# Larger place tiles and earlier expert loads, quarters moved from GpSimd to VectorE, and smaller batches at both ends of a long gather, in a two-block transformer kernel

## The chip, the core and the metric

The kernel runs on one core of one Trainium2 chip, as one program. The metric is device time in microseconds, taken by the clock of the chip. Five engines work side by side: TensorE (PE in the profile, with its weight loads as PEld), VectorE (DVE), ScalarE (ACT), GpSimd (POOL) and SyncE (SP, here used only to issue DMAs). Each engine takes its own instructions strictly in the order in which they are written, and waits where a semaphore has not reached its value.

## The reference

Two transformer blocks on 256 tokens of width 1024, one layer each, everything in fp32. What matters here is the second half of each block.

```python
# block 1: hierarchical mixture of experts, 4 groups of 8 experts, 2 experts for each token
h = h + hierarchical_moe(rmsnorm(h), ...)
#   for each expert e: silu(x @ w_gate[e]) * (x @ w_up[e]) @ w_down[e], weighted by the token's gate
#   w_gate, w_up: 32 x 1024 x 512, w_down: 32 x 512 x 1024  (2 MB each, 192 MB in all)
x = rmsnorm(h, final_norm_g)
...
# block 2, last part: product keys pick 16 of 16384 experts for each of 8 heads of a token
q = (xt @ w_q); s = q . sub_keys; top 16 of each half, then top 16 of the 256 sums
act = gelu(x . u_tab[expert]); out = sum_k gate_k * act_k * v_tab[expert_k]
```

The last part reads 128 rows of `u` and of `v` (4 KB each) for each of the 256 tokens.

## The kernel before

The program is written engine by engine, and the order on an engine is the order of the text. There are five stages: `mixers_*` (block 1's attention and gating), `experts_*` (its experts), `mixers2_*` and `cross_*` (block 2 up to the cross attention), and `peer_*` (its product key experts). Nothing is scheduled by a planner. Each stage has counters (`m_pe`, `p_dve` and so on), and a wait names a step of a counter.

**Weights.** Each piece of weights is a 2 MB load into one of seven slots of 16 KB for each partition (`piece`, `load_piece`, L138 to L171). Pieces have a fixed order, `load_order`; SP issues them, and waits first for the piece `behind` places earlier to have landed, so that two or three are under way. `high_quarters` (ScalarE, L173 to L178) rounds a piece to fp32r in four quarters of 1024 columns, and `low_quarters` (L180 to L185) takes the rest, raw minus rounded, on VectorE or on GpSimd. A product of fp32 accuracy is then three fp32r products (`three`).

**Experts.** At most 64 tokens use an expert, each in a slot. `PG` holds, for the four experts of a group of four, a 0/1 matrix from tokens to slots. For each of the 32 experts TensorE runs gate (32 matmuls of 256 columns in two halves of the array), up (the same), the sums of the expert before into the tokens (`add`), the slots' gates (`gate_of_slots`), two transposes of the hidden values, the turned `PG`, for the first 28 experts a part of the next group's gather, and down (`y`). VectorE copies the slots' gates (L841), multiplies silu by up (L843, `h`) and splits; ScalarE does silu (L732), the copy `hp` (L734) and the scaled result `ysh` (L738). Pieces are `eg`, `eu`, `ed` (gate, up, down) for each expert; expert piece j goes into the slot that piece j-7 leaves, so SP also waits for TensorE's step of piece j-7. The first seven are issued once TensorE has finished the mixers (`r11`). `b0` to `b3` are the first pieces of block 2. `b0` waits for step `y29` and for `eu31` to have landed, `b1` for `gate30` and `ed31`. The quarters of `b0` are rounded around the work on expert 31.

**Product key experts.** `select(n)` on VectorE finds the 32 experts of the two heads n%4 of token half n//4; its outer sums are L1922, and its result `idx{n}` (L1955). TensorE computes 16 query units `q0` to `q15` (4 for each of `pq0` to `pq3`), each 24 matmuls, and keys from them. A gather g (GpSimd, L2045) fetches for each of 128 tokens row `IDX[:, g]` of `uv` (8 KB, 1 MB in all) into one of 14 places of a ring. Gather 2 waits for `q7`, 6 for `q11`, 12 for `q15`, and a gather that reuses a place for the row that lay there to have been summed; gathers 8 to 11 reuse the places of 0 to 3. For each batch of four rows VectorE takes the dot products (`dots`, L1892), ScalarE gelu (L1808), weights (L1813) and diagonal matrices (`DG`, L1819), and TensorE adds the rows (`add_rows_pe`, two fp32 matmuls of 512 columns for each row). Batch 0 is added between `q11` and `q12`, all others after `q15`. After the last row come a norm and the stores.

## Time and profile before

| | us |
|---|---|
| median of 3 runs (1681.23 to 1686.05) | 1681.42 |
| profiled execution, its own time | 1684.5 |
| its span | 1682.7 |
| TensorE busy | 1468.9 (87%) |
| VectorE busy | 790.7 (47%) |
| ScalarE busy | 465.2 (28%) |
| bytes read from HBM | 541.87 MB, 323 GB/s over the span |

The chain that ended last has 54% of its time on PE and 24% on DMA. These shares are an average over stages with different limits: the experts run from 155.7 to 630.5 us of the span, the gather stage from about 1003 us to the end, and what binds differs. A row of a timeline gives the start, the time to the end of the group, engine, line, tiles, how many instructions were merged, and in brackets the idle time before it and who ended that.

### The profile page before, as it was taken

Reading aid. Unit: us, or ns where it says so; the run is one execution under the profiler, and the core shown is the slowest. Engines: PE = TensorE matmul, PEld = TensorE weight load, DVE = VectorE, ACT = ScalarE, POOL = GpSimd, SP = SyncE. Lnnn points to the kernel's source line nnn. Section 1 sums busy time; section 2 is a strip of 40 time slices with the busy share of each in tenths; the row PEclk is TensorE's granted clock in tenths of the full one; section 3 lists DMA queues with packets and bytes.
Section 4 is the critical chain, followed back from the end, with each engine's and each line's share of the span. In section 5 each row is a group of like instructions: output and inputs, shape, how many; then the busy total and the mean of one; then the engine's idle time right before and its main releaser. Section 6 shows DMA issues by size and latency. Waiting matters only on the chain.

```text
span 1682.7 us, 19564 instructions
## 1 busy us (share of the span) xinstructions
PE 1468.9 (87%) x7830; PEld 903.3 (54%) x7830; DVE 790.7 (47%) x1821; ACT 465.2 (28%) x1173; POOL 271.6 (16%) x280
## 2 busy tenths in 40 slices
PE   7998999999999989999999888878787777877776
PEld 7777555555555549976668686333332333333332
DVE  5535111111111125256464476576776677545443
ACT  4621100110101024355533443222222222222221
POOL 0001000000000000000000033433333333433330
PEclk8999999999999999989999998989989998999998
DMA  8209999999999983522234218999999999999993
GB/s 341 101 1 398 425 426 425 424 424 425 427 423 425 424 352 115 214 102 100 101 150 150 110 67 325 422 421 422 422 420 423 421 422 421 421 422 423 422 421 162
DMA packets 63055, 544.24 MB, mean 323 GB/s; under 512 B 6384, under 2 KB 6896, under 8 KB 10096
## 3 DMA queue, kind: packets, MB, share of 16 engines
q1 hardware_dynamic: 25664, 273.31, 39.4%
q0 software_dynamic: 36864, 268.45, 38.5%
q8 instruction: 63, 1.03, 0.2%
q10 hardware_dynamic: 432, 1.18, 0.2%
q14 instruction: 32, 0.26, 0.0%
HBM read 541.87 MB, written 1.05 MB: 323 GB/s over the span
## 4 chain that ended last, share of the span: by engine, by line
PE 54%; DMA 24%; DVE 9%; issue 8%; ACT 4%; POOL 1%; SPq 0%; ACTq 0%; DVEq 0%; POOLq 0%
PE PS L189 52%; DMA AR<-in_uv,CO 19%; DMA Wk<-in_uv,CO 4%; DVE AR L1892 2%; PE PS L199 2%; ACT Wk L1813 1%; DMA CO<-in_const 1%; DVE AR L843 1%; ACT AR L1819 0%; DVE AR L1922 0%; DVE XL L259 0%; DVE Wk L1892 0%; DVE Wk L841 0%; DVE LO L185 0%; ACT XH L252 0%
## 5 line engine op out<-in xcount | busy, mean ns | idle before, releaser
L189 PE MATMUL PS<-AR 128*64 128x256 f32 (+3 forms) x2784 | 633.2, 463 | 122.0 <-ACT AR L1819 120.3
L189 PEld LDWEIGHTS PS<-AR 128*64 128x64 f32 (+3 forms) x2784 | 308.6, 160 | 449.8 <-issue 227.8
L1892 DVE CUSTOM_DVE_ANT_0 AR<-AR,PS 128x1024 f32<-128x1024 f32 x218 | 263.6, 1219 | 199.7 <-DMA AR<-in_uv,CO 199.1
L2045 POOL DMA_INDIRECT AR<-in_uv,CO x218 | 207.5, 952 | 336.1 <-PE PS L189 327.3
L280 POOL TENSOR_TENSOR ST<-ST 128x2 f32<-128x2 f32 (+3 forms) x12 | 10.3, 860 | 904.1 <-DVE ST L263 904.1
L189 PE MATMUL PS<-AR,Wk 128*64 128x512 f32 (+4 forms) x592 | 148.7, 565 | 4.3 <-ACT Wk L734 1.4
L185 DVE TENSOR_TENSOR LO<-AR,HI 128x1024 fp32r<-128x1024 f32 x100 | 118.0, 1232 | 64.1 <-ACT HI L178 64.1
L189 PE MATMUL PS<-Wk,AR 128*64 128x256 f32 (+2 forms) x488 | 113.7, 451 | 20.8 <-ACT AR L1819 20.2
L1808 ACT ACTIVATE Wk<-Wk 128x4 f32<-128x4 f32 x64 | 13.1, 205 | 423.6 <-DVE Wk L1892 423.6
L189 PE MATMUL PS<-XH,HI 128*128 128x256 f32 x352 | 104.0, 295 | 10.3 <-DVE XL L259 7.0
L178 ACT ACTIVATE HI<-AR 128x1024 fp32r<-128x1024 f32 x104 | 102.5, 1053 | 16.1 <-PE PS L189 9.4
L841 DVE COPY Wk<-PS 128x1 f32<-128x1 f32 x32 | 5.1, 158 | 211.0 <-PE PS L189 211.0
L189 PE MATMUL PS<-XL,HI 128*128 128x256 f32 x352 | 101.4, 288 | 0.0
L189 PE MATMUL PS<-XH,LO 128*128 128x256 f32 x352 | 101.2, 288 | 0.0
L189 PEld LDWEIGHTS PS<-Wk,AR 128*64 128x64 f32 (+1 forms) x488 | 56.5, 164 | 75.6 <-issue 38.2
L189 PEld LDWEIGHTS PS<-AR,Wk 128*64 128x64 f32 (+2 forms) x592 | 53.9, 151 | 77.9 <-issue 68.0
L189 PE MATMUL PS<-HI,XH 128*128 128x512 f32 (+1 forms) x208 | 85.0, 409 | 3.8 <-ACT AR L1303 2.7
L1819 ACT ACTIVATE AR<-CO,Wk 128x128 f32<-128x128 f32 x256 | 81.8, 390 | 2.1
L189 PE MATMUL PS<-LO,XH 128*128 128x512 f32 (+1 forms) x208 | 82.0, 394 | 0.0
L189 PE MATMUL PS<-HI,XL 128*128 128x512 f32 (+1 forms) x208 | 81.8, 393 | 0.0
L189 PEld LDWEIGHTS PS<-XH,HI 128*128 128x128 f32 x352 | 69.4, 197 | 11.9 <-DVE XL L259 6.9
L851 DVE SCALAR_TENSOR_TENSOR YL<-PS,Wk,YH 128x512 fp32r<-128x512 f32 x32 | 24.0, 750 | 110.1 <-ACT YH L738 110.1
(263 smaller groups left out, 1684.8 us busy)
## 6 DMA issues: line engine op xcount, KB each, us to landing
AR<-in_w_gate SPq DMA_DIRECT2D x28, 2048.0 KB, 13.1
AR<-in_w_up SPq DMA_DIRECT2D x27, 2048.0 KB, 14.1
AR<-in_w_down SPq DMA_DIRECT2D x27, 2048.0 KB, 14.7
AR<-in_w_in SPq DMA_DIRECT2D x15, 2048.0 KB, 9.9
Wk<-in_w_up SPq DMA_DIRECT2D x5, 2048.0 KB, 14.7
Wk<-in_w_down SPq DMA_DIRECT2D x5, 2048.0 KB, 14.7
AR<-in_w_out SPq DMA_DIRECT2D x4, 2048.0 KB, 8.0
Wk<-in_w_gate SPq DMA_DIRECT2D x4, 2048.0 KB, 12.8
```

Source lines behind the costliest of these rows:

```text
L178: act.activation(hi[:, cs], w[:, cs], ACT.Copy).then_inc(*steps.up(f"{name}.{k}"))
L185: eng.tensor_tensor(lo[:, cs], w[:, cs], hi[:, cs].bitcast(F32), ALU.subtract).then_inc(*steps.up(f"{name}.{k}"))
L189: return pe.matmul(o, l, r, start=start, stop=stop, skip_group_check=True)
L199: return pe.transpose(o, i, ident[0:n, 0:n])
L280: pool.tensor_tensor(ST[:, a:b], ST[:, a:b], HALF[:, 0:b - a], ALU.pow).then_inc(*rms.up(site))
L843: dve.tensor_tensor(HM[:, b, :], SG[:, b, :], P(4 + b)[:, 256:512], ALU.mult).then_inc(*m_dve.up(f"h{ex}"))
L851: dve.scalar_tensor_tensor(YL[:, b, :], P(6), SLOT_GATE[:, b:b + 1], YH[:, b, :].bitcast(F32), ALU.mult, ALU.subtract).then_inc(*m_dve.up( ...
L1808: act.activation(GEL[:, cs], DT[:, cs], ACT.Gelu).then_inc(*a_own.up())
L1813: t = act.activation(WT[:, g:g + 1], BGf[:, g:g + 1], ACT.Copy, scale=GEL[:, g:g + 1])
L1819: act.activation(DG[:, g % 8, :], ident, ACT.Copy, scale=WT[:, g:g + 1]).then_inc(diags, 1)
L1892: t = dve.tensor_tensor_reduce(r, r, P(6 if g < 128 else 2, 2), 1.0, 0.0, ALU.mult, ALU.add, DT[:, g:g + 1])
L2045: pool.indirect_dma_start(RING[k], None, uv, bass.IndirectOffsetOnAxis(ap=IDX[:, g:g + 1], axis=0)).then_inc(g_in[k], 16)
```

## The change

Ten edits, in four places.

1. **Loads.** The seven pieces of the mixers use other slots and halves, so that slots come free earlier. `eu0` is issued at step `k3`, `out0` and `out1` one step later than before, `eg0` at `u1`, `eu1` at `turn2.3`, `ed0` and `ed1` at `r01`, `eg1` and `eg2` at `r11`. The expert loop issues from `eu2` on.
2. **Start.** TensorE's spare matmuls wait for the identity matrix, whose rounded copy now lies in `WM`; 20 of them instead of 36 stand first.
3. **Experts.** `PG` holds each expert's 64 slots twice, so that turning it and summing the gates take one matmul of 128 output rows instead of two of 64; the turned `PG` is an fp32r product with the rounded identity instead of an fp32 one. VectorE does `h` before the slots' gates, and down waits for the gates.
4. **Expert 31.** Two quarters of `b0` are rounded between `hp31` and `ysh31` (before: three ahead of silu31, one after `hp31`), two after `ysh31`. Of the rests, two stand ahead of `ys31` and two after block 2's first scaling.
5. **Gather stage.** The rests of `pq2` move from GpSimd to VectorE, behind `select(0)`; `exp0` moves from behind `q7`'s keys to behind `q11`'s, and `gates0` behind the first batch of dots. Batches are 2, 2, 61 times 4, 2, 2, 1, 1, 1, 1 rows instead of 64 times 4.

```diff
-            piece(name, src, n % 4, n % 2)
+            piece(name, src, (2, 3, 0, 1, 2, 0, 1)[n], (n + 1) % 2)
...
-            sp.wait_ge(*a_pe.at("k3"))
-            load_piece(sp, "out0")
-            sp.wait_ge(*a_pe.at("v1"))
-            load_piece(sp, "out1")
+            for name, step in (("eu0", "k3"), ("out0", "v1"), ("out1", "g1"), ("eg0", "u1"), ("eu1", "turn2.3"), ("ed0", "r01"),
+                               ("ed1", "r01"), ("eg1", "r11"), ("eg2", "r11")):
+                sp.wait_ge(*a_pe.at(step))
+                load_piece(sp, name, 2 if name in ("out0", "out1") else len(load_order))
...
-            spare(pe, 6, 36)
+            spare(pe, 6, 20)
...
-            sp.wait_ge(*a_pe.at("r11"))
-            for ex in range(32):
+            for ex in range(2, 32):
...
-                    pg = PG[:, g % 2, tt, k4 * 64:k4 * 64 + 64].bitcast(F32)
-                    for j in range(2):
-                        t = mm(pe, G[64 * j:64 * j + 64, 256 + tt * 128:384 + tt * 128], pg, ident, True, True)
+                    t = mm(pe, G[:, 256 + tt * 128:384 + tt * 128], twice(PG[:, g % 2, tt, k4]), WMt[:, 0:128], True, True)
...
                 if ex == 31:
-                    act.wait_ge(*m_pe.at("gate31"))
-                    high_quarters(act, "b0", b_act, range(3))
...
-                    high_quarters(act, "b0", b_act, range(3, 4))
+                    high_quarters(act, "b0", b_act, range(2))
                 act.wait_ge(*m_pe.at(f"y{ex}"))
                 act.activation(YH[:, b, :], P(6), ACT.Copy, scale=SLOT_GATE[:, b:b + 1]).then_inc(*m_act.up(f"ysh{ex}"))
+            high_quarters(act, "b0", b_act, range(2, 4))
             high_quarters(act, "b1", b_act)
...
-            low_quarters(pool, "pq2", p_act, p_pool)
...
+            low_quarters(dve, "pq2", p_act, p_dve)
             low_quarters(dve, "pq3", p_act, p_dve)
             dots(dve)
+            gates(dve, 0)
...
+        SIZES = [2, 2] + [4] * 61 + [2, 2, 1, 1, 1, 1]
+        STARTS = [sum(SIZES[:b]) for b in range(len(SIZES) + 1)]
```

On TensorE in the first expert, behind the gate and up matmuls: the slots' gates (`Wk,PG`), the two transposes (L199), the turned `PG`, the gather and down. Before:

```order
L189 MATMUL PS<-Wk,PG 64x1 x4
L199 MATMUL PS<-CO,AR 128x128 [waits m_dve]
L199 MATMUL PS<-CO,AR 128x128
L189 MATMUL PS<-CO,PG 64x128 x4
L189 MATMUL PS<-PG,XGH 128x256 [waits m_dve]
```

After:

```order
L189 MATMUL PS<-Wk,PG 128x1 x2
L199 MATMUL PS<-CO,AR 128x128 [waits m_dve]
L199 MATMUL PS<-CO,AR 128x128
L189 MATMUL PS<-WM,PG 128x128 x2
L189 MATMUL PS<-PG,XGH 128x256 [waits m_dve]
```

Two of four instructions are gone in each of two places, and the turned tile reads `WM` instead of `CO`.

On ScalarE around expert 31 (L732 and after L730 are silu, L734 and L732 `hp`, L738 and L736 `ysh`; `HI_49` is `b0`, `HI_50` is `b1`; ring0 and ring1 are their landings). Before:

```order
L178 ACTIVATE HI_49<-AR 128x1024 [waits ring0,m_pe]
L178 ACTIVATE HI_49<-AR 128x1024 x2
L732 ACTIVATE AR<-PS 128x256 [waits m_pe]
L734 ACTIVATE Wk<-PS 128x256 [waits m_pe]
L178 ACTIVATE HI_49<-AR 128x1024 [waits ring0]
L738 ACTIVATE YH<-PS,Wk 128x512 [waits m_pe]
L178 ACTIVATE HI_50<-AR 128x1024 [waits ring1]
L178 ACTIVATE HI_50<-AR 128x1024 x3
```

After:

```order
L730 ACTIVATE AR<-PS 128x256 [waits m_pe]
L732 ACTIVATE Wk<-PS 128x256 [waits m_pe]
L178 ACTIVATE HI_49<-AR 128x1024 [waits ring0]
L178 ACTIVATE HI_49<-AR 128x1024
L736 ACTIVATE YH<-PS,Wk 128x512 [waits m_pe]
L178 ACTIVATE HI_49<-AR 128x1024 [waits ring0]
L178 ACTIVATE HI_49<-AR 128x1024
L178 ACTIVATE HI_50<-AR 128x1024 [waits ring1]
L178 ACTIVATE HI_50<-AR 128x1024 x3
```

The first wait for `b0` stands behind `hp31` now, and two quarters stand ahead of `ysh31`.

On ScalarE in the gather stage, from the keys of `q7` on (L1838 and after L1841 copy keys, L1848 and L1851 queries, L1824 and L1827 are `exp0`, `HI_49` is `pq3`). Before:

```order
L1838 ACTIVATE AR<-PS 128x2x128 [waits p_pe] x2
L1824 ACTIVATE RW<-RW 128x32 [waits p_dve]
L178 ACTIVATE HI_49<-AR 128x1024 [waits ring3]
L178 ACTIVATE HI_49<-AR 128x1024 x3
L1848 ACTIVATE RW<-PS 128x256 [waits p_pe] x2
L1838 ACTIVATE AR<-PS 128x2x128 [waits p_pe]
```

After:

```order
L1841 ACTIVATE AR<-PS 128x2x128 [waits p_pe] x2
L178 ACTIVATE HI_49<-AR 128x1024 [waits ring3]
L178 ACTIVATE HI_49<-AR 128x1024 x3
L1851 ACTIVATE RW<-PS 128x256 [waits p_pe] x2
L1841 ACTIVATE AR<-PS 128x2x128 [waits p_pe]
```

`exp0`, which waits for VectorE's `sub0`, no longer stands ahead of the quarters of `pq3` and of the copies of `q8` and `q9`.

## Rows read from the trace of the kernel before

**Rows 1.** Busy time by stretch: span, engines (instructions), granted clock, DMA share, GB/s.

```profile
200.00:300.00 100.00, 95.88 (x780) 57.29 (x778) 18.99 (x46) 9.51 (x20) 0.00 (x0) 1.00 1.01 426
```

**Rows 2.** Timeline of PE, inside one expert's period.

```profile
413.90 0.40 PE L189 MATMUL PS<-Wk,PG 128*64 128x1 f32 x8
414.89 0.51 PE L199 MATMUL PS<-CO,AR 128*128 128x128 f32 x2 [0.59 <-DVE AR L843]
415.32 0.66 PE L189 MATMUL PS<-CO,PG 128*64 128x128 f32 x8
```

**Rows 3.** Timeline of ACT and of DVE, the same expert.

```profile
412.89 0.39 ACT L732 ACTIVATE AR<-PS 128x256 f32<-128x256 f32 x1 [6.22 <-PE PS L189]
...
414.42 0.41 DVE L843 TENSOR_TENSOR AR<-AR,PS 128x256 f32<-128x256 f32 x1
```

**Rows 4.** Timeline of SP: issues of pieces, first and last of the experts.

```profile
127.32 0.33 SPq L171 DMA_DIRECT2D AR<-in_w_gate  x1
...
135.30 0.33 SPq L171 DMA_DIRECT2D AR<-in_w_gate  x1
...
159.42 0.33 SPq L171 DMA_DIRECT2D AR<-in_w_up  x1
...
603.19 15.32 SPq L171 DMA_DIRECT2D AR<-in_w_in  x4
```

**Rows 5.** Page, groups of instructions: busy us, mean ns, idle before.

```profile
L185 DVE TENSOR_TENSOR LO<-AR,HI 128x1024 fp32r<-128x1024 f32 x100 | 118.0, 1232 | 64.1 <-ACT HI L178 64.1
...
L178 ACT ACTIVATE HI<-AR 128x1024 fp32r<-128x1024 f32 x104 | 102.5, 1053 | 16.1 <-PE PS L189 9.4
```

**Rows 6.** Timeline of PE and of DVE, end of the experts.

```profile
621.52 3.65 PE L189 MATMUL PS<-Wk 128*64 128x512 f32 x16 [0.48 <-ACT Wk L734]
626.75 0.50 PE L189 MATMUL PS<-YH,PT 64*128 64x512 f32 x2 [1.57 <-DVE YL L851]
...
627.99 2.48 DVE L857 TENSOR_TENSOR Hs<-PS,Hs 128x512 f32<-128x512 f32 x4 [1.29 <-PE PS L189]
```

**Rows 7.** Timeline of POOL and of DVE around the selection of the first experts.

```profile
984.73 9.55 POOL L185 TENSOR_TENSOR LO<-AR,HI 128x1024 fp32r<-128x1024 f32 x4 [20.78 <-ACT HI L178]
...
986.82 7.49 DVE L1922 TENSOR_TENSOR AR<-CO 128x32 f32<-128x32 f32 x7
...
1031.99 0.68 DVE L1922 TENSOR_TENSOR AR<-CO 128x32 f32<-128x32 f32 x7
```

**Rows 8.** Timeline of POOL, gathers 0, 2 and 12.

```profile
1003.15 1.17 POOL L2045 DMA_INDIRECT Wk<-in_uv,CO  x1 [8.88 <-DVE RW L1956]
...
1006.54 1.96 POOL L2045 DMA_INDIRECT AR<-in_uv,CO  x1 [0.30 <-issue]
...
1042.30 0.94 POOL L2045 DMA_INDIRECT AR<-in_uv,CO  x1 [11.44 <-PE PS L189]
```

**Rows 9.** Timeline of ACT and of PE between keys 7 and batch 0.

```profile
996.88 0.38 ACT L1838 ACTIVATE AR<-PS 128x256 f32<-128x256 f32 x1 [0.36 <-PE PS L189]
1002.99 0.23 ACT L1824 ACTIVATE RW<-RW 128x32 f32<-128x32 f32 x1 [5.72 <-DVE RW L1956]
...
1016.05 0.38 ACT L1848 ACTIVATE RW<-PS 128x256 f32<-128x256 f32 x1 [2.48 <-PE PS L189]
...
1020.83 5.40 PE L189 MATMUL PS<-Wk,AR 128*128 128x512 f32 x8 [3.62 <-ACT AR L1819]
```

**Rows 10.** Timelines of DVE, ACT and PE at the last rows.

```profile
1662.93 1.22 DVE L1892 CUSTOM_DVE_ANT_0 AR<-AR,PS 128x1024 f32<-128x1024 f32 x1 [1.23 <-DMA AR<-in_uv,CO]
...
1664.43 0.85 ACT L1813 ACTIVATE Wk<-RW,Wk 128x1 f32<-128x1 f32 x4
...
1655.92 7.13 PE L189 MATMUL PS<-AR 128*128 128x512 f32 x16 [1.12 <-ACT AR L1819]
1665.77 8.83 PE L189 MATMUL PS<-AR 128*128 128x512 f32 x16 [2.71 <-ACT AR L1819]
...
1674.64 1.29 DVE L1976 TENSOR_TENSOR Hs<-PS,Hs 128x512 f32<-128x512 f32 x2 [10.48 <-PE PS L189]
```

More of the change, by code:

```diff
@@ L576, in program @@
         XG = w2(4096, "p (b c n) -> p b c n", b=2, c=8)
-        PG = rounded("PG", "Wk", wk.at, 1024)[:, :].rearrange("p (b t n) -> p b t n", b=2, t=2)
-        wk(1024)
+        PG = rounded("PG", "Wk", wk.at, 2048)[:, :].rearrange("p (b t e d s) -> p b t e d s", b=2, t=2, e=4, d=2)
+        wk(2048)
+        twice = lambda v: v.rearrange("p d s -> p (d s)")
         HP = wk(512, "p (b n) -> p b n", b=2)
@@ L690, in experts_pe @@
                 for tt in range(2):
-                    pg = PG[:, g % 2, tt, k4 * 64:k4 * 64 + 64].bitcast(F32)
-                    for j in range(2):
-                        t = mm(pe, G[64 * j:64 * j + 64, 256 + tt * 128:384 + tt * 128], pg, ident, True, True)
+                    t = mm(pe, G[:, 256 + tt * 128:384 + tt * 128], twice(PG[:, g % 2, tt, k4]), WMt[:, 0:128], True, True)
                 t.then_inc(*m_pe.up(f"turned{ex}"))
@@ L790, in places_dve @@
             b = g % 2
-            slot = bc(io[:, 0:64].unsqueeze(1), [128, 4, 64])
+            slot = bc(io[:, 0:64].unsqueeze(1).unsqueeze(1), [128, 4, 2, 64])
             for tt in range(2):
-                pg = PG[:, b, tt, :].rearrange("p (e s) -> p e s", e=4)
-                dve.tensor_tensor(pg, slot, bc(RK[:, tt, 4 * g:4 * g + 4].unsqueeze(2), [128, 4, 64]), ALU.is_equal).then_inc(
+                own_slot = bc(RK[:, tt, 4 * g:4 * g + 4].unsqueeze(2).unsqueeze(3), [128, 4, 2, 64])
+                dve.tensor_tensor(PG[:, b, tt], slot, own_slot, ALU.is_equal).then_inc(
                     *m_dve.up(f"pg{g}.{tt}"))
@@ L837, in experts_dve @@
                     places_dve(dve, g + 1)
-                if ex == 31:
-                    low_quarters(dve, "b0", b_act, b_dve, range(2))
+                dve.wait_ge(*m_act.at(f"silu{ex}"))
+                dve.tensor_tensor(HM[:, b, :], SG[:, b, :], P(4 + b)[:, 256:512], ALU.mult).then_inc(*m_dve.up(f"h{ex}"))
                 dve.wait_ge(*m_pe.at(f"gsum{ex}"))
                 dve.tensor_copy(SLOT_GATE[:, b:b + 1], P(5 - b)[:, 0:1]).then_inc(*m_dve.up(f"gs{ex}"))
-                dve.wait_ge(*m_act.at(f"silu{ex}"))
-                dve.tensor_tensor(HM[:, b, :], SG[:, b, :], P(4 + b)[:, 256:512], ALU.mult).then_inc(*m_dve.up(f"h{ex}"))
                 dve.wait_ge(*m_act.at(f"hp{ex}"))
@@ L848, in experts_dve @@
                 if ex == 31:
-                    low_quarters(dve, "b0", b_act, b_dve, range(2, 4))
+                    low_quarters(dve, "b0", b_act, b_dve, range(2))
                 dve.wait_ge(*m_act.at(f"ysh{ex}"))
@@ L1362, in mixers2_dve @@
             scaled(dve, XZ[:, 1, :], H[:, 1, :], ST[:, 1:2]).then_inc(*b_dve.up("xs1"))
+            low_quarters(dve, "b0", b_act, b_dve, range(2, 4))
             turn_dve(dve, X2, sm["g_nmix"], b_act, b_dve, "x")
@@ L1691, in program @@
         p_act = Steps(sem("p_act"), [*p_act_names, *[f"exp{n}" for n in range(1, 8)]])
-        p_dve = Steps(sem("p_dve"), ["ss", "mean", "xs1", *eights("x"), "idx0", "sub0", "gates0", *split_steps("pq3"),
+        p_dve = Steps(sem("p_dve"), ["ss", "mean", "xs1", *eights("x"), "idx0", "sub0", *split_steps("pq2"), *split_steps("pq3"), "gates0",
                                      *[f"{k}{n}" for n in range(1, 8) for k in ("idx", "sub", "gates")]])
-        p_pool = Steps(sem("p_pool"), split_steps("pq2"))
         ld_sk, ld_gp, ld_fin, st_out = sem("ld_sk"), sem("ld_gp"), sem("ld_fin"), sem("st_out")
@@ L1753, in peer_sp, with batch @@
             sp.wait_ge(st_out, 48)
+        SIZES = [2, 2] + [4] * 61 + [2, 2, 1, 1, 1, 1]
+        STARTS = [sum(SIZES[:b]) for b in range(len(SIZES) + 1)]
+        def batch(b):
+            return range(STARTS[b], STARTS[b + 1])
         def sums_at(tt, j):
@@ L1758, in add_rows_pe @@
         def add_rows_pe(pe, b):
-            for g in range(4 * b, 4 * b + 4):
+            for g in batch(b):
                 tt, n = g // 128, g % 128
@@ L1800, in peer_pe @@
                     add_rows_pe(pe, 0)
-            for b in range(1, 64):
+            for b in range(1, len(SIZES)):
                 add_rows_pe(pe, b)
         def weights_act(act, b):
-            cs = slice(4 * b, 4 * b + 4)
+            cs = slice(STARTS[b], STARTS[b + 1])
             act.wait_ge(dotted, b + 1)
             act.activation(GEL[:, cs], DT[:, cs], ACT.Gelu).then_inc(*a_own.up())
-            if b % 8 == 0:
-                act.wait_ge(*p_dve.at(f"gates{b // 8}"))
+            act.wait_ge(*p_dve.at(f"gates{(STARTS[b + 1] - 1) // 32}"))
             act.wait_ge(*a_own.at())
-            for g in range(4 * b, 4 * b + 4):
+            for g in batch(b):
                 t = act.activation(WT[:, g:g + 1], BGf[:, g:g + 1], ACT.Copy, scale=GEL[:, g:g + 1])
@@ L1815, in weights_act @@
             act.wait_ge(*a_own.at())
-            for g in range(4 * b, 4 * b + 4):
+            for g in batch(b):
                 if g >= 8:
@@ L1851, in peer_act @@
                 keys(hc)
-                if ui == 1:
+                if ui == 2:
                     exp_act(act, 0)
-                if ui == 2:
                     weights_act(act, 0)
-            for b in range(1, 64):
+            for b in range(1, len(SIZES)):
                 if b in DOTTED_AT_SUB:
@@ L1888, in dots @@
             b = batches.count
-            for g in range(4 * b, 4 * b + 4):
+            for g in batch(b):
                 r = RING[place_of[g]][:, 0:1024]
@@ L2007, in peer_dve @@
             mean(dve, ST[:, 40:41], D).then_inc(*e_dve.up("mean0"))
-            while batches.count < 64:
+            while batches.count < len(SIZES):
                 dots(dve)
```

23 lines of the change are left out of this document (12 added, 11 removed).

## The prediction

> **What bounds the kernel now.** I read the busy table by stretches first, since the whole span mixes several limits. In a stretch of 100 us inside the experts TensorE is busy for 95.9 us at the full granted clock, and the 16 DMA engines are busy throughout (share 1.01) at 426 GB/s [rows 1]. So two limits lie on each other: a change that shortens TensorE's work gains only until the transfers bind. Next I read TensorE's timeline inside one expert for the parts that are not weights [rows 2], then SP's issues, which tell when pieces land [rows 4]. At the end of the experts the two are apart: the last piece, `ed31`, landed at 608.2 us (`b1` waits for it; the four issues from 603.19 on are 5.0 us apart), while TensorE began the product with it only at 621.52 and ended at 625.2 [rows 4, 6]. TensorE binds there, with 13 us of cover over the transfers. In the gather stage the page's rows are of DMA: 256 gathers of 1 MB, each 2.5 us, so what counts is when the stream starts, whether it has a gap near its start, and how long the tail behind the last row is. The start hangs on `idx0`, and just ahead of it stands the row that surprised me: seven small outer sums took 7.49 us on VectorE, and the same seven take 0.68 us in the next selection. They end with GpSimd's four quarters (984.73 + 9.55 = 994.28 against 986.82 + 7.49 = 994.31) [rows 7].
>
> The sums are made in the profiled execution: span 1682.7, own time 1684.5, against a median of 1681.42. I take differences from its span and put them on the median.
>
> **Experts, TensorE's side.** The slots' gates are 0.40 us for eight instructions, four calls; two calls are left, so I take 0.2 off. TensorE then waits 0.59 for `h` before the transposes; `h` could start when silu is done (412.89 + 0.39 = 413.28) but stood behind the gates' copy until 414.42 [rows 2, 3]. With the order turned, `h` runs 413.3 to 413.7, ahead of the end of the slots' gates at 414.1, and the wait goes; next late there is nothing but TensorE itself. The turned `PG` starts at 415.32 and what follows it comes 0.59 later; two fp32r calls should cost between nothing less (0.59, if an fp32r product of 128 columns is as slow as four fp32 calls) and 0.12; I take 0.2, so 0.4 off, nearer to the fp32r rows. Sum 1.2 us for each expert, bounds 0.8 and 1.3, times 32 = 38 us (25 to 42). This alone would end the experts at 625.2 - 38 = 587. The wait of down for the gates' copy costs nothing: VectorE does it right behind `h`, and the copy `hp` takes as long.
>
> **Experts, the transfers' side.** From the landing of the first piece (135.30, 8.0 after its issue) to that of the last (608.2) are 95 pieces in 472.9 us, 4.98 us each [rows 4]. Early loads cannot run further ahead than seven slots. Before, the seventh piece was landing when TensorE gave its first slot back (159.42, step `gate0`) [rows 4], and the stream did not pause. After, the seven lie ready and the stream rests until that step: the eighth piece lands 8.0 after it, at 167.4, and the last, 88 pieces on, at 167.4 + 88 x 4.97 = 604.8. I add 0.3 for the start: twice two place tiles of 512 columns instead of 256 on the way to the first gather are some +0.6 (bounds 0 and 0.8), and the spare matmuls, which begin later but end nearer to the first weights, I take at -0.3 (bounds -2 and +1). So `ed31` lands at 605.1 instead of 608.2. All the loading early is worth 3 us; the mixers' own later loads of `out0` and `out1` are hidden, since each is issued some 10 us ahead of its first quarter and lands in 8. TensorE (587) is ahead of it, so in the last third TensorE waits for pieces, and **the transfers bind**.
>
> **The end of the experts.** `y31` would end at about 609. But `b0` lands 5.0 behind `ed31`, at 610.1, and ScalarE now waits for it between `hp31` and `ysh31`. Two quarters at 1.0 [rows 5] give 612.1, `ysh31` 612.8; VectorE's two quarters at 1.2 (from 611.1) end at 613.5, `ys31` at 614.2; the last sums take 1.2 at the full clock, and at half of it 2.3 (TensorE has idled for 5 us; the row before shows full clock behind an idle of 1.57 [rows 6]); I take 2.3. Then four additions of 2.48 [rows 6] end at 619.1 against 630.5. **Gain 11.4 us** (12.5 with the full clock; 14 if `b0` did not stand in the way; 9 if pieces take 5.0). The two quarters of `b0` behind `ysh31` and `b1`, which lands at 615.1, end on ScalarE at 619.0, just in time for the norm. The two rests behind the first scaling take 2.4 and fit an idle of 3 us of VectorE's there.
>
> **Start of the gathers.** GpSimd's quarters go. If they held the outer sums, `idx0` comes 7.49 - 0.68 = 6.8 us earlier, at 996.2, and gather 0 is issued at 996.4 instead of 1003.15 [rows 7, 8]. VectorE does the eight rests (9.3 us) by 1005.5. `q8` starts with the first of them at 997.4, `q11` is 13.5 later at 1010.9 instead of 1016.0 [rows 9]: before, the copy of `q8` stood behind `exp0`, which waited for VectorE until 1002.99, and behind four quarters. Batch 0's rows on TensorE start at 1015.3 instead of 1020.83; `exp0`, the table load and `gates0` now stand between, some 3 us; two rows take 5.4 of a cold clock, where four took 8.8 [rows 9]. So they end at 1020.7 instead of 1029.7, and `q15` is done at 1033.1 instead of 1042.1. **But the stream does not go on then**: gather 10 reuses the place of row 2, and row 2 is in batch 1 now, which TensorE adds only after `q15`. I put row 2 at 1037.5 to 1039.0, so gather 10 is issued about 4.0 ahead of where gather 12 was (1042.30 [rows 8]); two gathers more stand behind the gap, +5.0, and a load of 0.5 MB that fell into the restart has passed, -1.2. Sum -0.2, bounds -1.5 and +2. I take **0**. From there the stream is as before.
>
> **The tail.** The last dot starts at 1662.93; four weights are 0.85, and the last 16 matmuls start at 1665.77 and take 8.83 (7.13 where the idle before was short) [rows 10]. With single rows, the diagonal of the last is ready at about 1665.1, but TensorE must first be done with the rows before: it needs 1.8 for a row and they come every 2.5. Counting from the batch ahead of the last eight, it runs without pause and ends at 1667.4 (that batch at the full clock) to 1669.2 (cold). Against 1674.6: **gain 6.3 us** (5.4 to 7.2). What follows is unchanged.
>
> Sum: -11.4 + 0 - 6.3 = **-17.7**, 1681.4 - 17.7 = **1663.7 us**.
>
> **A rule weighed against the trace.** The row of the outer sums shows a VectorE instruction with two inputs in SBUF that lasts as long as a GpSimd one beside it [rows 7]. The Trainium skill, SBUF — State Buffer, "Who interferes with whom", states that such an instruction contends with a GpSimd instruction that reads SBUF; here the trace agrees, 7.49 against 0.68 us. The same page ("SBUF: two separate sides") warns that GpSimd, locked out, cannot write the descriptors of its own DMAs; by it moving the quarters to VectorE starves the first gathers, which is the second rival below. Its list of consequences exempts `tensor_tensor` from that as inferred.
>
> **Rivals.**
> *A. The transfers do not bind; TensorE does* (the fp32r products bring nothing and the wait for `h` stays in part). Then the experts gain 32 times the saving. At 0.3 us that is 10 us less the 2 of the late `ysh31`: total about -14, 1667. Against it: `h` is free 0.8 us before it is needed. 0.07.
> *B. The first gathers are starved by VectorE's rests.* GpSimd's issue took 1.17 and 1.96 us beside four rests, 0.94 alone [rows 8]: slowed, not stopped. If they wait until the rests end (1005.5), gather 1 lands some 8 us later, at 1014, batch 0 is dotted at 1015, its rows start 4 us later and so does everything behind: -13.7, 1667.7. 0.08.
> *C. The outer sums stay long, or the restart behind gather 10 is slower.* The start is then up to 7 us worse: -11, 1671. 0.10.
> *D. More than forecast*: no cold clock at the last sums, pieces at 4.93: -21.5, 1660 or below. 0.15.
> *E. Slower than before: the granted clock falls in the experts.* Once the transfers bind, TensorE waits some 1.4 us in every expert, some 14 times. In the gather stage a wait of 2.71 went with 8.83 instead of 7.13 [rows 10]. Each us at half clock costs 0.5, and 1.5 us of slack for each expert absorbs 3. From 6 us of half clock in each of 14 experts (14 x (3.0 - 1.5) = 21) the gain is gone, and at half clock throughout (14.9 of 14.9, 14 x 6 = 84) the kernel takes 1748. Against it: waits of 1.12 did not lower it [rows 10], and a TensorE that falls behind no longer waits. 0.03.
> *F. The change does not do what it says in full*: the transfers' gain is lost again before the gathers, and only the tail stays: -6, 1675; or a place wait that I missed eats that too, 1681. 0.05.
>
> **How the numbers follow.** The forecast has 0.52, with 1659 to 1668. The range reaches over B to most of C and D: 1657 to 1671. A measurement of this kernel tells 0.3% (5 us) from no change. Faster by more than that, below 1676.4: the forecast, A, B, C, D and half of F, 0.945, of which I take 0.065 off for what I have not seen: 0.88. Within: the other half of F, 0.025, and 0.045 of that, 0.07. Slower: E and the rest, 0.05.
>
> **What would show it.** Right: in the first half of the experts a period of about 13.6 us on TensorE, in the last third 14.9 with waits for a DMA of about 1.4; the first half-rounding of `b0` near 610 with `ysh31` behind it, and the residual additions at 619; seven outer sums in 0.7; the first gather at 985 (996.4 - 11.4); a gap of the stream after gather 9; the last rows in pieces of 1.8. Wrong: no waits for pieces, a clock below 1.00 among the experts, the first gather's issue far behind `idx0`, or a second gap in the stream.

## The result, and the profile after

| | before | changed |
|---|---|---|
| runs beside each other, median (lowest to highest) | 1683.2 us (1681.23 to 1686.05, 4 runs) | 1666.92 us (1664.19 to 1670.09, 4 runs) |
| ratio, 95% interval | | 0.991 (0.9889 to 0.9931) |
| span of the profiled execution | 1682.7 | 1666.0 |

The changed kernel is 16.3 us faster by the medians and 16.7 by the profiled spans. The forecast was 17.7 less.

The busy table by stretches of the changed kernel, with the columns of [rows 1] (busy of PE, PEld, DVE, ACT and POOL, granted clock, DMA share, GB/s):

```profile
140.00:150.00 10.00, 9.33 (x55) 8.99 (x54) 5.96 (x53) 2.62 (x9) 0.00 (x0) 0.69 0.00 0
200.00:300.00 100.00, 100.00 (x772) 60.69 (x770) 20.96 (x47) 10.18 (x21) 0.00 (x0) 1.00 1.01 426
400.00:500.00 100.00, 92.33 (x690) 54.02 (x691) 20.38 (x45) 9.80 (x20) 0.00 (x0) 1.00 1.01 424
...
1015.00:1020.00 5.00, 5.00 (x45) 5.00 (x43) 4.86 (x24) 0.77 (x2) 0.00 (x0) 1.00 0.54 200
1020.00:1025.00 5.00, 4.97 (x42) 4.72 (x40) 4.79 (x10) 1.53 (x4) 0.00 (x0) 1.00 0.02 6
1025.00:1030.00 5.00, 3.43 (x6) 1.47 (x5) 3.45 (x8) 4.56 (x16) 0.00 (x0) 0.68 0.29 104
1030.00:1035.00 5.00, 5.00 (x13) 2.15 (x12) 0.00 (x0) 2.11 (x3) 2.95 (x4) 0.98 0.54 174
```

In the first half of the experts TensorE is busy throughout, in the second half it is busy for 92 of 100 us, at the same full clock and the same transfer rate. It waits for pieces now. Two stretches have idle transfers: 140 to 150, where the seven early pieces lie ready, and 1015 to 1035, the gap behind gather 9.

TensorE's timeline of the changed kernel: two transposes of successive experts in the first half (start, us, tiles), and gate and up of one expert in the second half, with the wait for `eu`.

```profile
207.06 0.47 PE L199 MATMUL PS<-CO,AR 128*128 128x128 f32 x2
220.72 0.46 PE L199 MATMUL PS<-CO,AR 128*128 128x128 f32 x2
...
419.75 3.62 PE L189 MATMUL PS<-AR 128*64 128x256 f32 x32
424.25 3.67 PE L189 MATMUL PS<-AR 128*64 128x256 f32 x32 [0.88 <-DMA AR<-in_w_up]
```

The period is 13.66 us instead of 14.77, and the wait of 0.59 for `h` [rows 2] is gone. From the seventeenth expert on it is 14.7 to 14.8, with three of 15.3 to 15.8, and most experts wait 0.8 to 1.2 us for a DMA (two of them 1.4 and 1.9).

To see where the time went, I cut each profiled execution at four events: the start of the first expert's gate on TensorE, the first scaling of block 2 on VectorE (the one behind the residual additions), the issue of gather 0 on GpSimd, and the start of the last dot. The stretches between them are differences of starts in the timelines.

```
us                to gate0   to scaling   to gather 0   to last dot   to the end   span
before             155.7       477.1        370.3         659.8         19.8      1682.7
changed            158.0       466.8        362.2         666.6         12.4      1666.0
n_late_loads       158.5       467.1        364.7         665.6         13.7      1669.6
n_old_turn         161.6       467.9        360.9         665.3         13.7      1669.3
n_old_turn_h       161.3       476.1        362.9         666.0         13.7      1679.9
n_b0_late          156.2       467.0        365.1         665.8         13.7      1667.8
n_pool_rests       157.7       466.3        367.4         661.4         12.4      1665.1
n_first4           155.8       468.0        361.3         663.2         13.8      1662.1
n_gate8            158.3       466.8        361.3         659.5         13.8      1659.6
n_tail4            161.2       466.2        364.7         665.8         18.2      1676.0
n_b0_b1_late       157.7       463.3        365.5         665.7         12.4      1664.6
n_old_start        158.2       465.9        358.9         665.1         13.7      1661.8
n_best             156.0       463.3        363.5         657.7         12.4      1653.0
n_best_start       155.8       463.2        365.6         658.0         13.5      1656.0
```

The table is read by column. A stretch in which two kernels have the same program still differs by up to 6 us in the first column (155.8 to 161.6 for the kernels with the changed start), by some 3 either way in the third, and by 1.4 in the last, all in single executions. The experts and the stream of gathers, which hang on transfers, repeat within about 2 us. So an effect of the experts is read from the second column and one of the gathers from the fourth, not from the spans.

### The profile page after: what moved, and what is told of

Same layout as the page of the kernel before. It is cut to its first block, busy times and chain, and to the rows that moved or that the text cites. A ratio compares the mean times of both kernels' runs of the same rounds, so it can differ in the third digit from the quotient of the medians.

```text
span 1666.0 us, 18993 instructions
## 1 busy us (share of the span) xinstructions
PE 1451.0 (87%) x7494; PEld 893.6 (54%) x7494; DVE 794.8 (48%) x1826; ACT 467.1 (28%) x1178; POOL 262.3 (16%) x276
## 4 chain that ended last, share of the span: by engine, by line
DMA 46%; PE 35%; issue 8%; DVE 6%; ACT 4%; POOL 1%; SPq 0%; ACTq 0%; DVEq 0%; POOLq 0%
PE PS L189 34%; DMA AR<-in_uv,CO 23%; DMA AR<-in_w_up 17%; DMA Wk<-in_uv,CO 3%; DMA Wk<-in_w_up 3%; DVE AR L1894 1%; PE PS L199 1%; ACT Wk L1816 1%; DMA CO<-in_const 1%; DVE LO L185 1%; DMA AR<-in_w_in 1%; POOL AR L2047 1%; ACT AR L1822 1%; DVE XL L259 0%; ACT Wk L1812 0%
## 5 line engine op out<-in xcount | busy, mean ns | idle before, releaser
L185 DVE TENSOR_TENSOR LO<-AR,HI 128x1024 fp32r<-128x1024 f32 x104 | 122.5, 1232 | 64.9 <-ACT HI L178 64.9
L1812 ACT ACTIVATE Wk<-Wk 128x4 f32<-128x4 f32 (+2 forms) x69 | 14.1, 205 | 423.7 <-DVE Wk L1894 423.7
L838 DVE TENSOR_TENSOR AR<-AR,PS 128x256 f32<-128x256 f32 x32 | 13.5, 421 | 201.7 <-ACT AR L730 201.7
L178 ACT ACTIVATE HI<-AR 128x1024 fp32r<-128x1024 f32 x104 | 102.5, 1053 | 17.2 <-DMA AR<-in_w_in 10.5
L730 ACT ACTIVATE AR<-PS 128x256 f32<-128x256 f32 x32 | 12.3, 384 | 231.1 <-PE PS L189 231.1
## 6 DMA issues: line engine op xcount, KB each, us to landing
AR<-in_w_gate SPq DMA_DIRECT2D x28, 2048.0 KB, 14.7
AR<-in_w_up SPq DMA_DIRECT2D x27, 2048.0 KB, 14.7
AR<-in_w_down SPq DMA_DIRECT2D x27, 2048.0 KB, 14.7
Wk<-in_w_up SPq DMA_DIRECT2D x5, 2048.0 KB, 14.7
Wk<-in_w_down SPq DMA_DIRECT2D x5, 2048.0 KB, 14.7
Wk<-in_w_gate SPq DMA_DIRECT2D x4, 2048.0 KB, 14.7
```

The costliest lines, as they stand in the source:

```text
L178: act.activation(hi[:, cs], w[:, cs], ACT.Copy).then_inc(*steps.up(f"{name}.{k}"))
L185: eng.tensor_tensor(lo[:, cs], w[:, cs], hi[:, cs].bitcast(F32), ALU.subtract).then_inc(*steps.up(f"{name}.{k}"))
L730: act.activation(SG[:, b, :], G[:, 0:256], ACT.Silu).then_inc(*m_act.up(f"silu{ex}"))
L838: dve.tensor_tensor(HM[:, b, :], SG[:, b, :], P(4 + b)[:, 256:512], ALU.mult).then_inc(*m_dve.up(f"h{ex}"))
L1812: act.activation(GEL[:, cs], DT[:, cs], ACT.Gelu).then_inc(*a_own.up())
```

## The experiments

Each is the changed kernel with one more edit. Where only one execution was taken, the verdict rests on its stretches.

**The early loads (n_late_loads).**

```diff
-            for name, step in (("eu0", "k3"), ("out0", "v1"), ("out1", "g1"), ("eg0", "u1"), ("eu1", "turn2.3"), ("ed0", "r01"),
-                               ("ed1", "r01"), ("eg1", "r11"), ("eg2", "r11")):
+            for name, step in (("out0", "v1"), ("out1", "g1"), ("eg0", "r11"), ("eu0", "r11"), ("ed0", "r11"), ("eg1", "r11"), ("eu1", "r11"),
+                               ("ed1", "r11"), ("eg2", "r11")):
...
-                load_piece(sp, name, 2 if name in ("out0", "out1") else len(load_order))
+                load_piece(sp, name, 2 if name in ("out0", "out1") else 3)
```

> The changed kernel, but all seven first expert pieces are issued when TensorE has finished the mixers, in their order, each when the piece three places earlier has landed; the mixers' slots stay as changed. Theory of the resting stream: in the changed kernel the seven pieces lie ready by 138 us and the transfers then rest until the first slot comes free at 161.7, so the last expert piece lands at 608.7. With the loads from 127.8 on, the first lands at 135.8, the stream does not pause, and the last lands at 135.8 + 95 x 4.97 = 607.9: the residual additions end at 621.5 to 622.5 as before (622.4), the total is within 1 us. Rival (the term of 3 us that the prediction gave the early loads): the additions end at 625.4 and the kernel is 3 us slower than the changed one.

SP's issues of pieces in the changed kernel, from the eighth on, and ScalarE's first rounding of `b0`, which waits for it to land; then the first and the eighth issue of this kernel and the same rounding:

```profile
161.71 0.33 SPq L171 DMA_DIRECT2D AR<-in_w_up  x1
165.16 0.38 SPq L171 DMA_DIRECT2D AR<-in_w_down  x1
171.37 0.33 SPq L171 DMA_DIRECT2D AR<-in_w_gate  x1
...
230.94 0.33 SPq L171 DMA_DIRECT2D AR<-in_w_up  x1
...
613.67 2.00 ACT L178 ACTIVATE HI<-AR 128x1024 fp32r<-128x1024 f32 x2 [3.60 <-DMA AR<-in_w_in]
```

```profile
127.55 0.33 SPq L171 DMA_DIRECT2D AR<-in_w_gate  x1
...
162.21 0.33 SPq L171 DMA_DIRECT2D AR<-in_w_up  x1
...
614.56 2.00 ACT L178 ACTIVATE HI<-AR 128x1024 fp32r<-128x1024 f32 x2 [3.67 <-DMA AR<-in_w_in]
```

Loading the seven pieces some 8 to 83 us earlier moved the landing of `b0` from 614.56 to 613.67. Counted from the first expert's start the scaling comes at 466.8 and at 467.1. The early loads alone are worth 0.3 to 0.9 us, which is less than the column's own scatter. The span of this kernel is 3.6 us longer, as the rival had it, but only 0.3 of that is in the experts; the rest is in stretches with the same program (0.5 at the start, 2.5 ahead of gather 0, 1.3 at the end, less 1.0 in the stream). What sets the end of the stream is the first slot that TensorE gives back (161.71, 162.21), and ahead of it the transfers either rest or have just enough to do.

**TensorE's savings (n_old_turn, n_old_turn_h).** The first turns `PG` by an fp32 product again, the second also puts the slots' gates ahead of `h`.

```diff
-                    t = mm(pe, G[:, 256 + tt * 128:384 + tt * 128], twice(PG[:, g % 2, tt, k4]), WMt[:, 0:128], True, True)
+                    t = mm(pe, G[:, 256 + tt * 128:384 + tt * 128], twice(PG[:, g % 2, tt, k4]).bitcast(F32), ident, True, True)
```

> The changed kernel, but the turned place tile is again an fp32 product with the identity (two instructions). Theory that the transfers bind the experts: TensorE's period in the first experts goes from 13.65 to 13.8 or 13.9 us, still under the 14.9 that three pieces take, and the additions end at 622.4 as in the changed kernel. Rival, that TensorE binds: 32 x 0.2 = 6 us later, 628.

> The changed kernel with the fp32 turned place tile and with the old order on VectorE (the slots' gates ahead of h). Theory: the period of TensorE becomes 13.65 + 0.2 + 0.6 = 14.45; TensorE then is nearly as slow as the transfers, y31 ends at 158.0 + 28 x 14.45 + 4 x 13.9 = 618, the additions end at 624.5 instead of 622.4 and the kernel is 2 us slower. If the wait for h were worth nothing: 622.4. If TensorE bound in full (1.1 us x 32, as before the change): the additions end at 630 or more.

Transposes of two successive experts, n_old_turn and then n_old_turn_h:

```profile
211.31 0.46 PE L199 MATMUL PS<-CO,AR 128*128 128x128 f32 x2
225.19 0.46 PE L199 MATMUL PS<-CO,AR 128*128 128x128 f32 x2
```

```profile
213.50 0.50 PE L199 MATMUL PS<-CO,AR 128*128 128x128 f32 x2 [0.58 <-DVE AR L840]
228.13 0.51 PE L199 MATMUL PS<-CO,AR 128*128 128x128 f32 x2 [0.58 <-DVE AR L840]
```

The periods are 13.88 and 14.63 (14.64 as a mean), against 13.66. So of the 1.11 us saved for an expert, the fp32r product gives 0.22, the order of `h` 0.76, and halving the instructions the rest, 0.13. With 13.88 TensorE still waits for pieces in the last twelve experts, and the scaling comes at 467.9 instead of 466.8: next to nothing. With 14.64 it binds to the end: no expert waits for a piece, and the scaling comes 9.3 later. I had expected 2: the period came out 0.19 above my 14.45, which is 6 us over 32 experts, and the remaining 1 is within the scatter. The order of two VectorE instructions is the part of the change that counts in the experts.

**The end of the experts (n_b0_late, n_b0_b1_late).** The first rounds all of `b0` behind `ysh31` and takes its rests behind the scaling. The second also moves the rounding of `b1` behind the norm's sum of squares.

```diff
-                if ex == 31:
-                    high_quarters(act, "b0", b_act, range(2))
...
-            high_quarters(act, "b0", b_act, range(2, 4))
-            high_quarters(act, "b1", b_act)
+            high_quarters(act, "b0", b_act)
...
             square_sum(act, H[:, 0, :], XS[:, 0, :], ST[:, 0:1]).then_inc(*m_act.up("sq2"))
+            high_quarters(act, "b1", b_act)
```

> The changed kernel, but all four quarters of b0 are rounded behind ysh31, and all its rests are taken behind block 2's first scaling. In the changed kernel ysh31 starts at 615.58, 2.0 after y31 has ended, since ScalarE waits for b0 (landed 613.67) and rounds two quarters; VectorE's rests hold ys31 until 617.04. Theory: ysh31 starts at 613.7, the additions end at 619.8 instead of 622.4; but b1's four quarters now end on ScalarE at 622.6 and the norm's sum of squares stands behind them, so that the normalised residual comes no earlier and the kernel gains 0 to 0.3 us. Rival: b1's quarters are early enough, and the kernel gains 2.6.

> The changed kernel with the four quarters of b0 behind ysh31, as in n_b0_late, and with b1's four quarters moved behind the norm's sum of squares on ScalarE. In n_b0_late the additions ended at 617.2, 461.0 us behind the first expert's start instead of 464.4, but the scaling of the norm started 467.0 behind it, as in the changed kernel (466.8): the gain had been given back to b1's quarters. Theory: now the scaling starts 463.2 to 463.8 behind the first expert's start, and 3 us reach the first gather. Rival: b1's quarters, between the two norms, hold the second norm instead, and nothing is gained.

ScalarE and VectorE at the end of the experts, changed kernel:

```profile
615.58 0.67 ACT L736 ACTIVATE YH<-PS,Wk 128x512 fp32r<-128x512 f32 x1
...
618.71 3.90 ACT L178 ACTIVATE HI<-AR 128x1024 fp32r<-128x1024 f32 x4 [0.57 <-DMA AR<-in_w_in]
...
617.04 0.74 DVE L848 SCALAR_TENSOR_TENSOR YL<-PS,Wk,YH 128x512 fp32r<-128x512 f32 x1
619.96 2.48 DVE L854 TENSOR_TENSOR Hs<-PS,Hs 128x512 f32<-128x512 f32 x4 [2.18 <-PE PS L189]
```

The same in n_b0_late:

```profile
611.99 0.69 ACT L734 ACTIVATE YH<-PS,Wk 128x512 fp32r<-128x512 f32 x1 [3.75 <-PE PS L189]
...
617.27 3.89 ACT L178 ACTIVATE HI<-AR 128x1024 fp32r<-128x1024 f32 x4 [0.81 <-DMA AR<-in_w_in]
621.07 1.04 ACT L266 ACTIVATE XSs<-Hs 128x1024 f32<-128x1024 f32 x1
...
614.76 2.48 DVE L850 TENSOR_TENSOR Hs<-PS,Hs 128x512 f32<-128x512 f32 x4 [1.30 <-PE PS L189]
...
622.23 0.17 DVE L263 TENSOR_SCALAR ST<-ST 128x2 f32<-128x2 f32 x1 [3.71 <-ACT XSs L266]
```

And in n_b0_b1_late, with TensorE behind the experts:

```profile
618.60 1.06 ACT L266 ACTIVATE XSs<-Hs 128x1024 f32<-128x1024 f32 x1 [0.81 <-DVE Hs L849]
...
619.66 3.88 ACT L178 ACTIVATE HI<-AR 128x1024 fp32r<-128x1024 f32 x4
...
626.06 1.15 ACT L1248 ACTIVATE AR<-Hs,ST 128x1024 f32<-128x1024 f32 x1 [1.01 <-POOL ST L280]
...
621.83 9.53 PE L189 MATMUL PS<-WM 128*128 128x256 f32 x58 [5.79 <-issue]
631.19 1.96 PE L199 MATMUL PS<-CO,AR 128*128 128x128 f32 x16
```

In the changed kernel `ysh31` stands behind two roundings, which began at 613.67, when `b0` had landed, and lasted 2.0 us, while `y31` ended at 613.8. Without them the additions begin 458.5 us behind the first expert's start instead of 462.0. But the norm does not: its sum of squares stands behind `b1`'s four quarters and VectorE waits 3.71 us for it. Only when `b1` moves too does the scaling come 463.3 behind the start instead of 466.8, 3.5 us earlier. This is not the gain of the kernel, for the next thing in the way is TensorE. Between the experts and block 2's transposes it has 58 spare matmuls. In the changed kernel they hold the transposes until 634.47, 3.4 us after the normed tokens are ready (631.1); here until 631.19, 4.0 us after (626.06 + 1.15 = 627.2), and in n_best 5.0 us. Counted from the first expert's start, block 2's first product comes at 476.1 here, 477.1 in n_best and 476.0 in n_best_start, and at 476.9 to 479.2 in the kernels that leave `b1` where it is (n_old_turn_h aside): a mean of 1.8 earlier, with ranges that overlap. How much of that reaches gather 0 the executions cannot tell: the stretch behind the scaling was 3.3 longer here than in the changed kernel, 1.3 in n_best and 3.4 in n_best_start. No run here takes the spare matmuls out.

**The rests of `pq2` (n_pool_rests).** `low_quarters(dve, "pq2", p_act, p_dve)` goes back to GpSimd, ahead of its gathers.

> The changed kernel, but the four rests of pq2 are back on GpSimd. Theory, that they hold VectorE's seven outer sums: the sums take 7.5 us instead of 0.68 and the first gather is issued at 993.8 instead of 987.0. q11 comes about 1 later than the changed kernel's, because q8 waits for GpSimd's rests (ready 984.7 to 985, before 993.8), so the restart of the stream behind gather 10, which hangs on q15 and on TensorE, moves by 0 to 2 us and the kernel is only 0 to 2 us slower. Rival: the whole 6.8 us reach the end. Second rival: the outer sums were long for another reason, and stay at 0.68.

The outer sums on VectorE, GpSimd's rests and gather 0 in this kernel; the outer sums and gather 0 in the changed one:

```profile
974.93 7.59 DVE L1925 TENSOR_TENSOR AR<-CO 128x32 f32<-128x32 f32 x7
...
972.83 9.50 POOL L185 TENSOR_TENSOR LO<-AR,HI 128x1024 fp32r<-128x1024 f32 x4 [20.76 <-ACT HI L178]
991.37 1.98 POOL L2048 DMA_INDIRECT Wk<-in_uv,CO  x1 [9.04 <-DVE RW L1959]
```

```profile
977.47 0.68 DVE L1924 TENSOR_TENSOR AR<-CO 128x32 f32<-128x32 f32 x7
...
987.00 1.98 POOL L2047 DMA_INDIRECT Wk<-in_uv,CO  x1 [30.94 <-DVE RW L1958]
```

The seven sums are back at 7.59 us: GpSimd's subtraction of two SBUF tiles did hold them. This is the contention that the Trainium skill (SBUF — State Buffer, "Who interferes with whom") states, and the experiment bears it out. Gather 0 comes 5.2 us later behind the scaling, yet the kernel ends at the same time: 661.4 us from gather 0 to the last dot instead of 666.6. The earlier start is lost in the gap, since ScalarE's copy of `q15`, on which the restart hangs, follows the end of the additions by 401.4 us here (1023.04 - 621.63) and by 401.6 in the changed kernel (1023.99 - 622.44).

**The gap of the stream (n_first4, n_gate8).** In n_first4 the first batch has four rows: `SIZES = [4] * 62 + [2, 2, 1, 1, 1, 1]`. n_gate8 has that too, and:

```diff
-        place_of = [g if g < 8 else g - 8 if g < 12 else ROUND[(g - 12) % 14] for g in range(256)]
+        place_of = [g if g < 8 else ROUND[(g - 8) % 14] for g in range(256)]
...
-                if g in (2, 6, 12):
+                if g in (2, 6, 8):
...
-                if ui == 2:
-                    add_rows_pe(pe, 0)
-            for b in range(1, len(SIZES)):
+            for b in range(len(SIZES)):
```

(gather 8 waits for `q15`, `ROUND` becomes `[*range(8, 14), *range(8)]`, and ScalarE's weights of batch 0 stand behind `q15` as well).

> The changed kernel, but the first two batches of two rows are one of four (as before the change); the small batches at the end stay. Theory: gather 10, issued at 1030.7 in the changed kernel, waits for row 2, which stands behind q15; with four rows in batch 0 gathers 8 to 11 are issued by 1016 and gather 12 at about 1027.8 behind q15, which comes 3.5 later than 1024.0. Gather 12 then lands some 6 us earlier than now, and the kernel is 4 to 6 us faster than the changed one. Rival: the cold clock of the four rows delays q15 so much that nothing is won (0).

> The changed kernel with four rows in batch 0, and in addition batch 0 is added after q15, not between q11 and q12, and gathers 8 to 13 take the six places that q15 frees, instead of 8 to 11 reusing places 0 to 3. Theory: TensorE goes from q11 to q12 without its wait of 3.1 us and without the rows, q15 comes at 1002 + 13.2 = 1015.2 instead of 1024.0, and gather 8 is issued at 1015.5, when gather 7 has just landed: the gap of the stream is 3 to 5 us instead of some 13 of a mean share of one half, gather 14 lands at about 1038 instead of 1046, and the kernel is 8 to 9 us faster than the changed one. Rival: TensorE, which now has eight rows to catch up, holds the places back and opens a second gap; then 4 us or less.

GpSimd's issues around the gap: gathers 9 and 10 of the changed kernel, 11 and 12 of n_first4, 7 and 8 of n_gate8.

```profile
1011.85 0.94 POOL L2047 DMA_INDIRECT Wk<-in_uv,CO  x1 [0.78 <-PE PS L189]
1030.66 0.94 POOL L2047 DMA_INDIRECT AR<-in_uv,CO  x1 [17.87 <-PE PS L189]
```

```profile
1015.10 0.94 POOL L2047 DMA_INDIRECT AR<-in_uv,CO  x1 [0.78 <-PE PS L189]
1027.47 1.16 POOL L2047 DMA_INDIRECT AR<-in_uv,CO  x1 [11.43 <-PE PS L189]
```

```profile
1002.74 0.94 POOL L2044 DMA_INDIRECT AR<-in_uv,CO  x1 [0.30 <-issue]
1015.06 0.94 POOL L2044 DMA_INDIRECT AR<-in_uv,CO  x1 [11.39 <-PE PS L189]
```

Busy table of n_gate8 in the gap:

```profile
1005.00:1010.00 5.00, 5.00 (x45) 5.00 (x44) 4.72 (x14) 1.15 (x3) 0.00 (x0) 1.00 0.93 383
1010.00:1015.00 5.00, 5.00 (x45) 5.00 (x43) 3.65 (x16) 0.94 (x3) 0.00 (x0) 1.00 0.04 18
1015.00:1020.00 5.00, 1.60 (x8) 1.06 (x7) 1.40 (x12) 4.43 (x13) 3.76 (x4) 0.89 0.78 275
```

From gather 0 to the last dot: 666.6 in the changed kernel, 663.2 with four rows (3.4 less; I had expected 4 to 6), 659.5 when nothing stands between `q11` and `q15` (7.1 less; expected 8 to 9). In n_gate8 two stretches of 5 us lack transfers (shares of 0.04 and 0.78), in the changed kernel four (0.54, 0.02, 0.29, 0.54). TensorE catches up with its eight waiting rows without a second gap: GpSimd waits for it once more, 7.43 us ahead of the gather issued at 1050.29, and the DMA share is 1.01 there.

**The last batches (n_tail4).** `SIZES = [2, 2] + [4] * 63`.

> The changed kernel, but the last batches are of four rows again. Theory: the last 16 matmuls start 2.8 us behind the last dot and take 7.1 or 8.8; from the start of the last dot to the end of the span 19.8 us as before the change instead of 12.4, so 7.4 slower (5.7 if they run at the full clock).

TensorE's and VectorE's last work, changed kernel and then n_tail4:

```profile
1636.70 3.70 PE L189 MATMUL PS<-AR 128*128 128x512 f32 x8 [1.12 <-ACT AR L1822]
...
1643.67 14.27 PE L189 MATMUL PS<-AR 128*128 128x512 f32 x32
...
1653.61 1.22 DVE L1894 CUSTOM_DVE_ANT_0 AR<-AR,PS 128x1024 f32<-128x1024 f32 x1 [1.23 <-DMA AR<-in_uv,CO]
...
1657.97 1.29 DVE L1978 TENSOR_TENSOR Hs<-PS,Hs 128x512 f32<-128x512 f32 x2 [3.13 <-PE PS L189]
```

```profile
1650.88 17.00 PE L189 MATMUL PS<-AR 128*128 128x512 f32 x32 [2.80 <-ACT AR L1822]
```

TensorE in n_first4, whose tail takes 13.8 us:

```profile
1631.42 5.40 PE L189 MATMUL PS<-AR 128*128 128x512 f32 x8 [2.81 <-ACT AR L1822]
```

With fours the rest behind the last dot's start is 18.2 us, with single rows 12.4 in four executions and 13.5 to 13.8 in eight others, before the change 19.8. TensorE has no pause in its last 32 matmuls in either. In the changed kernel they take 14.3 us, with a granted clock of 1.00; in n_tail4 they begin behind a wait of 2.80 and take 17.0, with 0.51 and 0.81 in the first two stretches of 5 us. Which of its two values the tail of single rows takes goes with the clock in the batch ahead of the last eight rows: its first eight matmuls took 3.70 us at a granted clock of 1.00 in the changed kernel, and 5.40 at 0.72 in n_first4, and the other executions fall into the same two groups. The single rows are worth 4.4 to 5.8 against n_tail4, whose 5.8 more than the changed kernel is the 5.7 expected for the full clock, and 6.0 to 7.4 against the kernel before.

**The start (n_old_start).** Spare matmuls multiply zeros again, 36 stand first, and the rounded identity lies in the second half of `WM`.

```diff
-            spare(pe, 6, 20)
+            spare(pe, 6, 36)
...
-            dve.tensor_copy(WMt[:, 128:256], zeros)
+            dve.tensor_copy(WMt[:, 0:128], zeros).then_inc(wm_set, 1)
             dve.wait_ge(ld_id, 16)
-            dve.tensor_copy(WMt[:, 0:128], ident).then_inc(wm_set, 1)
+            dve.tensor_copy(WMt[:, 128:256], ident).then_inc(wm_set, 1)
```

> The changed kernel, but the spare matmuls multiply zeros again and 36 of them start first without waiting for the identity; the rounded identity lies in the second half of WM. In all nine profiles with spares on the identity the granted clock is 0.66 to 0.86 between 140 and 150 us, where it was 1.00 before the change, and the first expert starts at 155.8 to 161.6 (before: 155.7). Theory that the spares' start or data lowers the clock: the clock at 140 to 150 is 1.00, the first expert starts at 155.5 to 156.5 plus 0.6 for the wider place tiles, and the kernel is 1 to 3 us faster than the changed one. Rival: the clock falls there by the phase of the stages and does so here too; then the first expert starts at 157 to 161 as in the others and nothing is gained.

The stretch ahead of the first expert in this kernel:

```profile
140.00:150.00 10.00, 9.32 (x54) 8.98 (x53) 5.96 (x53) 2.62 (x9) 0.00 (x0) 0.68 0.02 7
```

The clock is as low as in the changed kernel (0.69), the first expert starts at 158.2, and the ratio to the kernel before is 0.9911 (0.9894 to 0.9927), that of the changed kernel. So it is neither the data nor the start of the spare matmuls. In n_late_loads the transfers ran through this stretch and it was 0.74, so it is not their rest either. TensorE was busy for 3.94 us of the 5 ahead of it (135 to 140) in the kernel before and in the changed one alike. Why the clock falls here in all thirteen executions looked at since the change (0.66 to 0.86) and did not in the one before stays open; with a single execution before, chance is not excluded.

**Together (n_best, n_best_start).** n_best has the edits of n_b0_b1_late and n_gate8; n_best_start has those of n_old_start too.

> The edits of n_b0_b1_late and of n_gate8 together. If they add up: 2.5 to 3.5 us at the end of the experts and 7 in the gather stage, that is 9.5 to 10.5 us less than the changed kernel, 1656 to 1657, ratio to the kernel before 0.984 to 0.986. Rival: the gap before q15 grows by what the experts give, no, q15 moves with them, so I see no way for it; a clock that falls elsewhere can cost 2 to 3.

> n_best with the old start of n_old_start. If the start costs 1 to 3 us, 1654 to 1656; if not, as n_best.

n_best: median 1656.29 (1654.80 to 1659.86, 4 runs) against 1679.47 of the kernel before beside it, ratio 0.9869 (0.9851 to 0.9887). n_best_start: 1658.88, 0.9885 (0.9868 to 0.9901). In the table n_best has both gains in their columns: 3.5 us to the scaling and 8.9 to the last dot. Its interval lies just below that of the changed kernel (0.9889 to 0.9931); the two ratios are 0.4% apart, some 7 us. I had expected 9.5 to 10.5, so the two gains do not add up in full: the 7 us are what n_gate8 alone gave from gather 0 on, and what n_b0_b1_late should add cannot be told from the scatter. The old start adds nothing.

## Why the prediction was right, and where its terms were off

- **Experts, TensorE's side.** 1.2 us for an expert were forecast, 1.11 came. The wait for `h` was the largest part, as said, and nothing took its place. The shares were off in opposite directions: `h` gave 0.76 where I had 0.59, the other edits 0.35 where I had 0.6.
- **Experts, the transfers' side.** That the transfers take over was right, with a period of 14.76 instead of 14.9 and waits of 0.8 to 1.2 instead of 1.4. But they did so from the seventeenth expert on, not only in the last third. The landing was mis-sized: `b0` at 613.7 instead of 610.1. Two things were left out. The eighth piece was issued at 161.7 and not at 159.7, since the first expert started 2.3 later and not 0.3, outside my bounds for the start (-2 and +1.8): TensorE's lower clock between 140 and 150 (0.69) was in no row of before. And the stream did not pick up at full rate: the next slots come free at 165.16 and 171.37, at TensorE's pace. The twentieth piece landed at 230.94 (the issue that waits for it), where 161.7 + 8.0 + 12 x 4.97 = 229.3; 1.6 us were lost there. So the 3 us that I gave to the early loads were not there: n_late_loads shows 0.3 to 0.9.
- **The end of the experts.** The step that `b0`'s landing holds `ysh31` was right in its mechanism, and each time behind it was late by the same 3.3 to 3.6: additions ended at 622.4 instead of 619.1, a gain of 8.0 and not 11.4. The last sums fell on a lower clock (0.72 between 615 and 620), as taken. That the wait costs only at the additions and not at the norm, because `b1` stands there, I had passed over as "just in time".
- **Start of the gathers.** 0.68 us for the outer sums, and gather 0 at 987.0: from the additions on 364.6 us instead of 372.7, 8.1 less, where I had 6.8. Then the term that mattered, that none of it survives gather 10's wait for row 2: the stretch to the last dot is 6.8 longer (666.6 against 659.8). In sum 1.3 us gained where I had taken 0, inside the stated bounds and inside the scatter of that stretch. n_pool_rests, n_first4 and n_gate8 show the mechanism from three sides.
- **The tail.** -7.4 in the profiled execution, just outside the forecast of -6.3 with 5.4 to 7.2; over the executions 6.0 to 7.4. The two ends that I gave, the batch ahead of the last eight rows at the full or the lower clock, are the two values that came.
- **Sum.** -8.0 - 1.3 - 7.4 = -16.7, against -11.4 + 0 - 6.3. Two terms were 1 us too small and one 3.4 too large, and that they partly cancel is luck: the total is nearer (16.7 to 17.7) than its largest term (8.0 to 11.4).
- **The rivals.** A needed a TensorE that binds to the end; n_old_turn_h is that kernel, and loses 9 us of the experts' gain. B (starved gathers): the first four issues took 1.98, 1.74, 1.97 and 1.97 us beside the rests instead of 0.94, slowed but not held. C (long outer sums): 0.68 us. D (pieces at 4.93): the period of 14.76 for three pieces is that rate, but a few late pieces and the slow pick-up took more than it gave. E (a falling clock among the experts): 1.00 between 200 and 600 us in spite of waits of 0.8 to 1.2.
